# Output projections of a hybrid decoder trunk by seven half-size products instead of eight

## What is computed

```python
xn = rmsnorm(h, norm_g);  z = xn @ w_in            # q, k, v, gates, pool input, merge gates
# gated linear attention and pooling give o (1024 wide) and y_pool (512 wide)
ya = o @ w_a;  yb = (y_pool * silu(gb)) @ w_b
s_a, s_b = split(sigmoid(mg + b_merge))
merged = s_a * ya + s_b * yb
h = h + merged @ w_out                              # w_out is 1024 x 1024
# for the sample group also, per sequence and head:
S_new = exp(bC) * S + kd.T @ v                      # S is 128 x 256, f32, read and written
```

## Time and profile before

| what | value |
|---|---|
| median of 3 runs | 1142.93 us (1142.36 to 1143.12) |
| profiled execution: span of the slowest core, core 6 | 1144.6 us |
| spans of the other seven cores | 1134.3 to 1143.4 us |
| granted TensorE clock, mean of each core | 0.989 to 0.995 |
| PE busy on core 6 | 1106.4 us (97%) |
| phase 2 of layer 0 / of layer 1, about | 330 to 592 / 890 to 1140 us |

### The profile page before, as it was taken

One profiled execution on the slowest core, in us unless ns is written; L12 is line 12 of the kernel. 1 busy time (PEld: TensorE's weight loads), 2 busy tenths in 40 slices (PEclk: granted clock), 3 DMA queues, 4 the chain that ended last, 5 costly groups with the idle time before them and its releaser, 6 DMA issues.

```text
span 1144.6 us, 27587 instructions; the slowest of 8 cores (1134.3 to 1144.6 us)
## 1 busy us (share of the span) xinstructions
PE 1106.4 (97%) x10010; PEld 860.7 (75%) x10010; DVE 611.3 (53%) x927; ACT 516.1 (45%) x1052; POOL 605.2 (53%) x903
## 2 busy tenths in 40 slices
PE   7899999999999999999999999999998999999997
PEld 3587777777788778777766877787787867787775
DVE  5447767755642544355344766766656244544433
ACT  2545566666333334334237365655543333434323
POOL 5258788866952334334342887787767323333232
PEclk8999999999999999999999999999999999999998
DMA  9965657685497999999889234445556946656321
GB/s 188 190 119 136 121 101 148 153 155 112 62 238 152 234 263 275 246 222 245 168 164 207 51 81 90 65 95 99 107 105 169 191 177 213 232 189 216 142 89 57
DMA packets 124361, 179.34 MB, mean 157 GB/s; under 512 B 82512, under 2 KB 89168, under 8 KB 120128
## 3 DMA queue, kind: packets, MB, share of 16 engines
q1 hardware_dynamic: 108960, 141.52, 43.6%
q0 software_dynamic: 15264, 36.05, 22.7%
HBM read 140.13 MB, written 54.59 MB: 170 GB/s over the span
## 4 chain that ended last, share of the span: by engine, by line
PE 80%; DMA 9%; issue 3%; POOL 3%; ACT 2%; DVE 2%; POOLq 0%; SPq 0%; DVEq 0%; ACTq 0%
PE psum L539 80%; DMA arena<-w 3%; ACT arena L566 2%; DMA arena<-arena 2%; POOL arena L581 2%; DVE arena L593 1%; DMA nsg_s<-arena 1%; DMA arena<-sgla 1%; DMA arena<-hin 1%; DMA OT<-arena 1%; POOL arena L588 1%; DVE arena L581 1%; DMA arena<-OT 0%; POOL arena L600 0%; PE psum L545 0%
## 5 line engine op out<-in xcount | busy, mean ns | idle before, releaser
L539 PE MATMUL psum<-arena 128*128 128x256 bf16 (+6 forms) x9906 | 1102.1, 279 | 28.7 <-DVE arena L593 7.7
L539 PEld LDWEIGHTS psum<-arena 128*128 128x128 bf16 (+2 forms) x9906 | 854.8, 98 | 271.4 <-issue 22.5
L581 POOL TENSOR_TENSOR arena<-arena 128x256 bf16<-128x256 f32 (+14 forms) x349 | 353.9, 1020 | 265.4 <-DVE arena L593 209.8
L593 DVE SCALAR_TENSOR_TENSOR arena<-arena,psum 128x256 f32<-128x256 f32 (+7 forms) x472 | 266.8, 601 | 301.3 <-ACT arena L566 151.9
L566 ACT ACTIVATE arena<-psum,arena 128x256 f32<-128x256 f32 (+3 forms) x432 | 173.2, 456 | 261.6 <-PE psum L539 207.1
L588 POOL TENSOR_SCALAR arena<-arena 128x256 f32<-128x256 f32 (+6 forms) x378 | 166.0, 448 | 186.9 <-ACT arena L566 125.3
L566 ACT ACTIVATE arena<-psum 128x256 bf16<-128x256 f32 (+5 forms) x258 | 159.1, 631 | 185.9 <-PE psum L539 159.3
L566 ACT ACTIVATE arena<-arena 128x1024 bf16<-128x1024 f32 (+4 forms) x144 | 141.7, 997 | 157.4 <-DVE arena L593 102.9
L593 DVE SCALAR_TENSOR_TENSOR arena<-arena 128x256 bf16<-128x256 f32 (+4 forms) x124 | 119.3, 970 | 52.5 <-POOL arena L581 51.2
L593 DVE SCALAR_TENSOR_TENSOR arena<-psum,arena 128x256 bf16<-128x256 f32 (+6 forms) x125 | 91.7, 755 | 57.6 <-PE psum L539 52.9
L613 POOL DMA_DIRECT2D arena<-w x106 | 62.5, 592 | 33.8 <-POOL arena L581 12.9
(11 more groups left out here) (10 smaller groups left out, 15.0 us busy)
## 6 DMA issues: line engine op xcount, KB each, us to landing
arena<-hin SPq DMA_DIRECT2D x32, 512.0 KB, 6.8
arena<-sgla SPq DMA_DIRECT2D x16, 1024.0 KB, 8.2
nsg_s<-arena SPq DMA_DIRECT2D x16, 1024.0 KB, 6.8
arena<-w POOLq DMA_DIRECT2D x30, 512.0 KB, 15.1
arena<-w POOLq DMA_DIRECT2D x48, 224.0 KB, 5.6
arena<-XN SPq DMA_DIRECT2D x20, 512.0 KB, 6.6
H<-arena SPq DMA_DIRECT2D x16, 512.0 KB, 6.1
arena<-H SPq DMA_DIRECT2D x16, 512.0 KB, 4.5
```

The lines of the kernel that those rows point to most:

```text
L539: return S.add("pe", lambda e: e.matmul(out, lhsT=lhsT, rhs=rhs, start=start, stop=stop, skip_group_check=sgc), r=[lhsT, rhs] + list(also_ ...
L581: return S.add(eng, lambda e: e.tensor_tensor(out=out, in0=in0, in1=in1, op=op), r=[in0, in1], w=[out], cost=c)
L593: return S.add("dve", lambda e: e.scalar_tensor_tensor(out=out, in0=in0, scalar=scalar, in1=in1, op0=op0, op1=op1), r=r, w=[out], cost=eco ...
```

## The change

The output projection of pairs 1 to 7 of phase 2's order (not of pair 0, nor of the last one of 80 or 64 rows) is no longer done tile by tile. `merged` of the pair is seen as 2 x 2 blocks a11, a12, a21, a22 (tile by half of the contraction), `w_out` as B11 to B22 (half of the contraction by column half), and the four blocks of the result come from seven products of 128 tokens x 512 x 512 instead of eight, with sums s1 to s4 of blocks of `merged` and T1 to T4 of blocks of `w_out`. Three products accumulate on one another in the bank "x", two in "y", and after each product the DVE adds half of the bank as it then stands to a half of h.

- `weight_sums` and `last_sums` make T1 to T4 once per layer, 16 DVE additions of 128x512 bf16; `merged_sums` makes s1 to s4 after the merge c = 7 of each pair, 4 such additions.
- `out_pair` gives four steps and a last one; `OUT_AT` says at which half merges of the next pair they come. A step at an even place comes between the gate matmuls and the other matmuls of a merge.
- In layer 0, T3 is written over B12 in place; the last tile there takes B12 as T1 + B11, four matmuls more.
- The room for T1 and T2 in layer 0 comes from the sample states, which are now 16 half units of 128x1024 f32 (one head, 512 KB) per layer: `S_in`, `S_bfm` and `kdm` are half as large. The counter spreads 36 units over the same 46 merges.
- Merges of pairs 2 and on, sample steps and products take the bank that has been free longest (`oldest`).

```diff
+OUT_AT = ((1, 3, 4, 5, 8), (0, 2, 3, 4, 5))
...
+        w12 = new_bf(4096)
+        S_in = [new_f32(1024) for _ in range(2)]
+        S_bfm = new_bf(1024)
         q_bd = new_bf(2048)
         xnO = new_bf(2048)
+        w4 = new_bf(512)
+        ms4 = [new_bf(512) for _ in range(2)]
...
         def sample_cast(l, u):
+            hp, j, i = u // 8, u // 2 % 4, u % 2
+            cp("act", S_bfm, S_in[u % 2])
+            h = 2 * hp + i
+            ts("pool", kdm[u % 2], ktok_m[:, h * 128:(h + 1) * 128], row_f[:, j:j + 1], s2=1.0, op1=ALU.mult)
 
         def sample_step(l, u, bo):
...
+            bs = [banks.oldest() for _ in range(4)]
             first = dict(also_r=[S_bfm, kdm[u % 2]], also_w=[bank(b) for b in bs])
             for r in range(4):
+                q_ = q_bd[:, (j * 4 + h) * 128 + 32 * r:(j * 4 + h) * 128 + 32 * r + 32]
+                mm(bank(bo)[32 * r:32 * r + 32, i * 256:(i + 1) * 256], q_,
+                   S_bfm[:, r * 256:(r + 1) * 256], j + i == 0, False, sgc=True, share=4.0, **first)
+                first = {}
+            for r in range(4):
+                p_ = slice(32 * r, 32 * r + 32)
+                mm(bank(bs[r])[:, 0:256], kdm[u % 2][p_, :], vtok_m[p_, h * 256:(h + 1) * 256], True, True, share=4.0)
+            for r in range(4):
+                s_ = slice(r * 256, (r + 1) * 256)
+                e = h * 16 + 4 * r + j
+                stt(S_in[u % 2][:, s_], S_in[u % 2][:, s_], ebcm[:, e:e + 1], bank(bs[r])[:, 0:256], ALU.mult, ALU.add)
                 banks.free(bs[r])
             dma(nsg_s[l, u], S_in[u % 2])
-            if u + 2 < 8:
+            if u + 2 < 16:
                 sample_load(l, u + 2)
...
+        def weight_sums(l, kc):
+
+            T1, T2, _, T4 = wsum[l]
+            tt("dve", T1[kc], wo(kc, 1), wo(kc, 0), ALU.subtract)
+            tt("dve", T2[kc], wo(kc + 4, 1), T1[kc], ALU.subtract)
+            tt("dve", T4[kc], wo(kc + 4, 0), T2[kc], ALU.subtract)
+
+        def last_sums(l, kcs):
+            for kc in kcs:
+                tt("dve", wsum[l][2][kc], wo(kc + 4, 1), wo(kc, 1), ALU.subtract)
...
+        def merged_sums(l, j):
+
+            a11, a12, a21, a22 = (merged_quarter(j, i, k) for i in range(2) for k in range(2))
+            s1, s2, s3, s4 = (V(s, 4, 128) for s in msum[l])
+            tt("dve", s1, a21, a22, ALU.add)
+            tt("dve", s2, s1, a11, ALU.subtract)
+            tt("dve", s3, a11, a21, ALU.subtract)
+            tt("dve", s4, a12, s2, ALU.subtract)
...
+            def product(name, a, w, i, b):
+                first = name not in box
+                if first:
+                    box[name] = banks.oldest()
+                for kc in range(4):
+                    mm(bank(box[name]), a[:, kc, :], w[kc], first and kc == 0, kc == 3, sgc=True)
+                q_ = h[i][:, b * 512:(b + 1) * 512]
+                stt(q_, bank(box[name]), 0.5, q_, ALU.mult, ALU.add)
...
+            def step0():
+                product("x", a11, B11, 0, 0)
+                product("z", a12, B21, 0, 0)
+                free("z")
+
+            def step1():
+                product("x", s2, T2, 0, 1)
+                product("y", s1, T1, 1, 1)
+
+            def step2():
+                product("x", s3, T3, 1, 1)
+
+            def step3():
+                product("y", s4, B22, 0, 1)
+                free("y")
+                out_done(l, j, 0)
+                product("x", a22, T4, 1, 0)
+                free("x")
+
+            return [step0, step1, step2, step3, lambda: out_done(l, j, 1)]
...
+                    if l == 0 and p == NPAIR and b and kc < 4:
+                        mm(bank(b_)[0:n, 512:1024], m_, wsum[0][0][kc], kc == 0, False)
+                        mm(bank(b_)[0:n, 512:1024], m_, wo(kc, 0), False, False)
+                        continue
...
+                at = OUT_AT[j == NPAIR] if j > 1 else ()
+                if at and c == 0:
+                    todo = out_pair(l, j - 1)
+                merge(l, j, c, todo.pop(0) if 2 * c in at else None)
+                if 2 * c + 1 in at:
+                    todo.pop(0)()
                 if j == 1 and c >= 6:
                     out_tile(l, 0, c - 6)
-                if j > 1 and c in (1, 3):
-                    out_tile(l, j - 1, c // 2)
+                if j == 1 and c >= 4:
+                    weight_sums(l, c - 4)
+                if (j, c) in ((1, 7), (2, 0)):
+                    last_sums(l, (2 - 2 * c // 7, 3 - 2 * c // 7))
+                if j < NPAIR and c == 7:
+                    merged_sums(l, j)
```

More of the change, by code:

```diff
@@ L514, in build_nc @@
         ypT.append(new_bf(1024))
-        kdm = [new_bf(256) for _ in range(2)]
+        kdm = [new_bf(128) for _ in range(2)]
+        o_msum1 = A_.top
         assert A_.top <= o_u
@@ L1220, in sample_step @@
         def sample_step(l, u, bo):
-            hp, j = divmod(u, 4)
-            bs = [banks.one() for _ in range(4)]
+            hp, j, i = u // 8, u // 2 % 4, u % 2
+            h = 2 * hp + i
+            bs = [banks.oldest() for _ in range(4)]
             first = dict(also_r=[S_bfm, kdm[u % 2]], also_w=[bank(b) for b in bs])
[L1225 to L1230, removed]
@@ L1284, in p2_loads, with merge @@
             dma(y_, YP[p], r=[("YP", p)])
-        def merge(l, j, c):
+        def merge(l, j, c, between=None):
             p = P2_ORDER[j]
@@ L1293, in merge @@
             W = cblock(c)
-            b_, c_ = banks.one(), banks.one()
-            ba, bb = bank(b_), bank(c_)
+            b_ = banks.oldest() if j > 1 else banks.one()
+            c_ = (banks.oldest() if j > 1 else banks.one()) if between is None else None
+            ba = bank(b_)
             for kc in range(8):
@@ L1308, in merge @@
             banks.free(b_)
+            if between:
+                between()
+                c_ = banks.oldest()
+            bb = bank(c_)
+            for kc in range(8):
+                mm(bb[:, 0:n], W[:, 2048 + kc * 128:2048 + (kc + 1) * 128], o3[:, kc, :], kc == 0, kc == 7)
+            for kc in range(4):
+                mm(bb[:, n:2 * n], W[:, 3072 + kc * 128:3072 + (kc + 1) * 128], y3[:, kc, :], kc == 0, kc == 3)
             stt(t_[:, 0:2 * n], e_[:, 0:2 * n], 1.0, bb[:, 0:2 * n], ALU.add, ALU.mult)
@@ new lines, in out_pair, with free @@
+        def out_pair(l, j):
+            k = 2 * j
+            h = [hb[(k + i) % 3] for i in range(2)]
+            s1, s2, s3, s4 = (V(s, 4, 128) for s in msum[l])
+            T1, T2, T3, T4 = wsum[l]
+            a11, a12, _, a22 = (merged_quarter(j, i, k_) for i in range(2) for k_ in range(2))
+            B11, B21, B22 = ([wo(kc + 4 * r, c) for kc in range(4)] for r, c in ((0, 0), (1, 0), (1, 1)))
+            box = {}
+            def product(name, a, w, i, b):
+                first = name not in box
+                if first:
+                    box[name] = banks.oldest()
+                for kc in range(4):
+                    mm(bank(box[name]), a[:, kc, :], w[kc], first and kc == 0, kc == 3, sgc=True)
+                q_ = h[i][:, b * 512:(b + 1) * 512]
+                stt(q_, bank(box[name]), 0.5, q_, ALU.mult, ALU.add)
+            def free(name):
+                banks.free(box.pop(name))
+            def step0():
[14 more added lines that the diff above has]
+            return [step0, step1, step2, step3, lambda: out_done(l, j, 1)]
@@ L1395, in step @@
             def step(u):
-                if u % 4 == 0:
+                if u % 8 == 0:
                     box[0] = banks.one()
                 sample_step(l, u, box[0])
-            for u in range(8):
+            for u in range(16):
                 units.append(lambda u=u: sample_cast(l, u))
                 units.append(lambda u=u: step(u))
-                if u % 4 == 3:
-                    units.append(lambda u=u: sample_o(u // 4, box[0]))
+                if u % 8 == 7:
+                    units.append(lambda u=u: sample_o(u // 8, box[0]))
             units.append(lambda: sample_gate(l))
-            done = 0
+            done, todo = 0, []
             total = 46
```

65 lines of the change are left out of this document (35 added, 30 removed).

## The result

The changed kernel takes 1150.18 us in the median of 10 runs, the kernel before 1143.03 beside it; the ratio is 1.0057 [1.0038, 1.0076]: some 7 us slower by the medians, 6.5 by the ratio. A second set gave 1154.18 against 1143.52, 1.0066 [1.0040, 1.0092]. The ratios leave disturbed runs out, so they differ a little from the quotients of the medians. The forecast was 1139.0 with a range up to 1147.0: wrong in sign, and outside the range. The profiled execution was one of the shorter ones, 1145.21 by the clock of the device with spans of 1133.2 to 1143.5 us per core. The execution of before had 1134.3 to 1143.4 and one core at 1144.6, so the spans alone hardly show the loss.

The account below looks back on a forecast made before the run. PE was taken to bound both second phases, almost without gaps. The terms -12.1 + 0.9 + 4.8 + 0.7 + 0.8 + 0.6 + 0.4 = -3.9 took 1142.9 to 1139.0 us, range 1134.5 to 1147.0.

Parts of the forecast that it names:

- Products removed: Second phases: 56 fewer 512-column matmuls at 0.2157 us, -12.1 us; four more in layer 0's last tile, +0.9.
- the saving is not what it seems: Rival, chance 0.02: removed matmuls give back only the skill's pitch, 4.4 us later, 1143.4.
- Half units: Sample states in both layers: 16 more half units, three tiling changes each at 0.1 us on PE, +4.8 us.
- Banks x and y: Products of a pair: PE waits until DVE has read x; slack 1.1 us, 0 to 11 us, taken 0.4.
- DVE is late for x: Rival, chance 0.17: at c = 0 to 2 of each pair, read-outs come late, 0.8 per pair, +6.9 us, 1149.8.
- Work added on DVE: Per pair +2.4 us of read-outs and +2.7 of sums at 0.685 each, beside PE; DVE busy 705 us.
- Weight sums: Early in phase 2, 11 us of DVE per layer; waits for pieces of Wo, 0 to 3 us, taken 0.7.
- State round trips: Layer 0's half units: 12.9 us store and load within 15, margin 5 to 2; from -1.3 to 6, taken 0.6.
- state trips come late: Rival, chance 0.12: about ten trips of layer 0 late by 1 us each on ACT, 4.7 instead of 0.6, 1143.1.
- Ends of the layers: After each layer's last full merge: PE waits 0 to 1.5 us per layer; -0.5 to 3 together, taken 0.8.

Follow-up runs that it names:

- The kernel with both moves put right: Changed kernel with the 256 KB load recorded behind its merge and the last pair's second transposing DMA and store tied behind the last merge: 1142.34 us, 0.9991.
- the square: Four kernels: changed (1.0057, 1.0066), with the tied load recorded early (1.0049), with the second transposing DMA and its store held later (1.0017), with both (0.9991).
- core 7 above: Core 7 of the changed kernel with only the 256 KB load recorded behind its merge: 1148.85 us, 1.0049; first large load landed in 24.1 us there.

## Why the prediction was wrong

By its own steps:

**Products removed**: right. 0.2157 us each gave 6.0 for layer 1, measured 6.6 by the ratio, 4.8 to 8.5 by its interval. The rule of about 131 ns ("TensorE: Matmul & The Clock Gate", Back-to-back issue gap, of the Trainium skill) would have given 28 x 0.131 = 3.7, below that interval; the row decided rightly. With it falls the rival that the saving is not what it seems.

**Half units**: the tiling changes were right, 5.1 for 4.8 predicted. All the waits were taken at 2.5 us together (0.7, 0.8, 0.6 and 0.4). With the end of layer 0 put right they come to some 5: -12.1 + 0.9 + 5.1 is -6.1, and that kernel measured -1.0 (3.4 to 6.9 by its interval). This mis-sizing alone would have left the time within the range.

**Banks x and y**: on core 5, PE's weight loads stand for DVE in layer 0 like this:

```profile
439.58 6.19 PEld L560 LDWEIGHTS psum<-arena 128*128 128x128 bf16 x44 [0.60 <-DVE arena L614]
446.91 1.09 PEld L560 LDWEIGHTS psum<-arena 128*128 128x128 bf16 x7 [1.13 <-DVE arena L614]
...
438.84 0.69 DVE L614 SCALAR_TENSOR_TENSOR arena<-psum,arena 128x512 f32<-128x512 f32 x1 [0.63 <-PE psum L560]
446.16 0.69 DVE L614 SCALAR_TENSOR_TENSOR arena<-psum,arena 128x512 f32<-128x512 f32 x1 [1.85 <-PE psum L560]
```

Each starts right behind the read-out of a product's bank. With a third at 406 us they make PE wait 1.4 us in layer 0, on every core, and nothing in layer 1: 1.4 in all, 0.1 per pair, where 0.4 in all was taken. The rival "DVE is late for x" needed 0.5 per pair: its mechanism exists, its size does not.

**Work added on DVE**: too high, harmlessly. The sums take 0.42 alone and 0.46 in the mean, not 0.685; DVE ends at 681.2, not 705. I had taken the one row of that shape and forgone the estimate of 0.42 from the Trainium skill ("VectorE: DVE Perf Modes", Mode 2x_1P), which the rows bear out. The read-outs take 0.691, as costed.

**Weight sums**: taken at 0.7, measured at nothing. DVE stood 0.74 us for a piece of Wo at 905.5 on core 5, and PE behind it on no core. **State round trips**: nearly. Stores and loads of the states land in 5.6 and 5.5 us in the median (for 6.1 and 6.8 taken), ACT stood 2.9 us for them in layer 0 on core 5, without PE behind it (on four other cores PE waited 0.3 to 0.7 us for ACT). In layer 1 one landed late, on core 5:

```profile
958.85 9.25 DMA arena<-sgla
...
968.18 1.07 ACT arena L587
...
969.38 160.69 PE psum L560 x1472
```

It cost PE 1.1 there, 0.7 and 0.2 on two more cores, nothing on the others. The rival "state trips come late" thus fails, but only by the bank choice: with the old one they and the banks cost over 20 us, which the prediction did not see; it weighed only the banks x and y.

**Ends of the layers**: the step that failed. The prediction priced them by PE, POOL and DVE at 0.8 for both layers, and counted it as a gain of up to 0.5 that the pair's end "lets the last norm start earlier". It followed the moved last step to its norm and not to what that issues. At the end of layer 0 the norm sends a transposing DMA and a store into SP's queue, and `pace` ties a weight load on POOL's queue to it. That the first is moved ahead of the large weight loads stands in no term of the sum; it and the tied load cost 7.5 to 8.6 us, where the term was 0.8. PE waits up to 7.8 us for the tied weights at the start of layer 1, and the granted clock stands at its lower level for up to 6.8 us with it.

The account, by ratios of 1143.6: products of layer 1 -6.6, half units +8.6, products of layer 0 -6.04 + 0.86 = -5.2 (by the sum, not measured alone), together -3.2. The kernel with both moves put right measured -1.0 (interval -2.7 to +0.8), so some 2 of small waits are left; its trace has 1.4 on DVE in layer 0 and, between the layers, 0.7 to 0.8 on ACT and 0.5 on DVE. The end of layer 0 adds 7.5 to 8.6 by the square. So even without it the change gives at most little: the half units, needed only for layer 0's sums, cost more than layer 0's products save.

The windows that I had read, 330 to 586 and 918 to 1120, end where the trouble begins. And a loss of 0 to 7.8 us, a different one on each core and in each execution, counts in a metric of the slowest core nearly by its largest.

## What to carry to other kernels

Follow a moved step through every instruction that it issues, into the queues: write down what each DMA was behind before and is behind now, and what is tied to "the operation recorded last". In this kernel the transposing DMA with its small packets belongs behind the large loads that the next stage waits for. Count a long wait of PE as more than its length: with the longest waits for weights the granted clock fell here. Price what an edit needs in order to fit (here half units in both layers for sums in one) apart from what it saves, and keep the part that pays: products in layer 1 alone take 1136.55 us, 0.9942 of the time before.

## What was not expected of the hardware

A 512 KB weight load that lands in 6.1 to 8.2 us beside one transposing DMA took 6.0 to 14.8 us, and once 24.1 (core 7 above), when two had been issued just ahead of it on another engine's queue. A change of the array's tiling cost 0.1 us, in whole and half units alike. With every single wait for weights of 3.3 us or more, in the two executions of the changed kernel, the granted clock fell to the lower of its two levels for 3.4 or 6.8 us, at the end of the wait or up to 3.5 us before it.
